# Two attention layers of a two-block transformer: heads in pairs, another order of steps, other PSUM banks, convolution taps loaded from DRAM

## The chip, the cores and the metric

The kernel runs on one core of a Trainium2 chip. The metric is the device time in microseconds of one execution; the kernel before was run three times.

## What is computed

Two transformer blocks run one after the other on 256 tokens of width 1024, in float32. The first block is not touched by the change. The second has two layers, and in each, between two gated feed-forward networks, there is a mixer:

```python
u_conv, q, k, v, q_mem = jnp.split(rms_norm_2(h, mix_norm[l]) @ w_in[l], splits, axis=-1)
y_conv = conv_module(u_conv, ...)      # gate, 31 causal taps per channel (384 channels), layer norm, silu
q = apply_rope(rms_norm_2(q), cos, sin)          # 6 query heads of 64, 2 key/value heads of 64
y_swa = sliding_window_attention(q, k, v, sinks) # blocks of 128, each sees itself and the one before
y_mem = memory_attention(rms_norm_2(q_mem), rms_norm_2(mk), mv)  # 4 heads of 64 over 256 memory rows
h = h + jnp.concatenate([y_conv, y_swa, y_mem], axis=-1) @ w_out[l]
```

## The kernel before, in words

Each engine has its own program in a fixed order, written by hand; semaphores named by `mark` and `at` tie them. All weights come as 268 units of at most 128x2048 floats through three slots. For a unit `u` SyncE loads `raw` when the low part of `u-3` is done, ScalarE writes the high part `w_hi` (`highs`, L888) when TensorE has finished unit `u-3`, VectorE writes the rest `w_lo` (`lows`, L1399), and TensorE multiplies high by high, low by high and high by low (`tile`, L286 to L288; `wide_tile`, L295 to L298; `rows_part`, L331 to L333). Each engine does its units in order, so a `highs` or `lows` call stands at one place in its program, and whatever is ahead of it delays it.

The mixer of a layer, from L706 on TensorE: three convolution units, query/key rows, value and memory-query rows, then memory keys and values. From there to the output projection TensorE alternates between small steps. There are ten heads (`WH`), 0 to 5 with the window, 6 to 9 over the memory:

- `window_scores(i)`: for both query blocks a bfloat16 mask matmul against the identity (L737, window heads only), then queries by keys (L738), on the 64 partitions of that head; a head's scores fill one bank, 0 or 1 by turns.
- VectorE `soft(i)`: row maxima of each query block (L1957, L1961) and the sink (L1964). ScalarE `soft(i)`: exponentials with their sums (L1317).
- `window_turned(i)`: transposes of the exponentials (L747) into bank 2 or 3; ScalarE copies them (L1325); `window_product(i)` multiplies by the values (L762).
- `third_channel(n)`: the convolution's third 128 channels, 31 taps, each a matmul of a diagonal 128x128 matrix with the shifted input (L776). ScalarE makes the diagonals from the identity, four after each head (`diagonals`, L1283), in a ring of eight. The other two thirds are 62 taps on VectorE (`run_taps`, L1916, L1920).

The lines that set the order in the ten rounds are, on ScalarE (behind `soft(i + 2)` and the four diagonals) and on VectorE:

```python
            if i in (1, 3):
                highs(u0 + L_MK + 3 + i // 2)
...
            run_taps(6)
            if i + 2 < WH:
                soft(i + 2)
            if i in (1, 3):
                lows(u0 + L_MK + 3 + i // 2)
```

After the last head, TensorE sums the convolution's channels (`conv_sums`, L828), transposes the memory heads' rows (`rows_turned`, L797), computes the variance (`conv_variance`, L835) and spreads its root (`spread`, L398), between the tiles of the output projection `L_WO`, four units of 16 tiles. The normalised convolution goes through VectorE and ScalarE as one piece of 128x768 (L2024 to L2034, L1372, L1376) and is what chunk 5 of the projection waits for.

## Time and profile before

| | us |
|---|---|
| median of 3 runs (lowest, highest) | 1743.68 (1743.01, 1745.07) |
| the profiled execution | 1742.12 |
| its span in the trace | 1740.8 |
| TensorE busy | 1683.9 |
| VectorE busy | 1232.8 |
| ScalarE busy | 892.8 |
| granted TensorE clock, share of full speed | 0.993 |

Spans and times in the trace count from the start of the profiled execution. A row of a timeline gives the start, the duration, the engine, the line, the operation, and in square brackets the idle time before it with what ended it. A float32 matmul stands as two passes, "x8" is four matmuls merged, and durations of neighbouring passes overlap by some 0.15 us, so what a group costs is read from the start of the next row. The first layer's mixer heads stand at 951 to 1005 us, the second's at 1458 to 1511 us.

### The profile page before, as it was taken

What the parts mean: (1) busy time and instruction counts of PE and PEld (TensorE: products, weight loads), DVE (VectorE), ACT (ScalarE), POOL (GpSimd) and SP (SyncE); (2) the same over time, 40 slices, a digit from 0 to 9 for tenths busy, and PEclk for the clock granted to TensorE, in tenths of its full rate; (3) what the DMA queues carried; (4) which work ended last, traced back from release to release, by engine and by line L of the source; (5) the groups of instructions that cost most, each with busy time, mean ns of one, the idle gap of its engine ahead of it and who ended that gap; (6) DMA issues with size and microseconds to landing.
All of it is one profiled execution on the core that took longest, in us unless ns stands there. A gap on an engine that the chain in (4) does not pass through costs nothing.

```text
span 1740.8 us, 24401 instructions
## 1 busy us (share of the span) xinstructions
PE 1683.9 (97%) x10136; PEld 1487.6 (85%) x10136; DVE 1232.8 (71%) x1487; ACT 892.8 (51%) x1149; POOL 183.2 (11%) x166
## 2 busy tenths in 40 slices
PE   7999999999999999999999899999999999899997
PEld 6889988888998888888889688888888898788886
DVE  7985577765657767677767767778777667677764
ACT  6554455444545554455444555556555545455542
POOL 0401010011101001100021010003100111010002
PEclk9999999999999999999999899999999999999999
DMA  7444345545434555555554215555555542145551
GB/s 280 162 160 143 120 165 194 191 179 211 159 112 166 194 210 182 186 183 190 194 179 149 73 57 210 194 200 189 179 196 187 194 172 107 49 149 189 184 197 55
DMA packets 41439, 291.09 MB, mean 167 GB/s; under 512 B 4720, under 2 KB 4976, under 8 KB 7024
## 3 DMA queue, kind: packets, MB, share of 16 engines
q1 hardware_dynamic: 39456, 282.61, 45.0%
q10 hardware_dynamic: 1872, 6.92, 1.0%
q8 instruction: 80, 1.31, 0.3%
q14 instruction: 31, 0.25, 0.0%
HBM read 288.46 MB, written 1.05 MB: 166 GB/s over the span
## 4 chain that ended last, share of the span: by engine, by line
PE 81%; DVE 11%; ACT 4%; POOL 2%; issue 2%; DMA 0%; ACTq 0%; DVEq 0%; POOLq 0%
PE ps L298 36%; PE ps L297 18%; DVE w_lo L1399 4%; PE ps L295 4%; PE ps L286 3%; PE ps L288 3%; PE ps L287 3%; PE ps L331 2%; PE ps L333 2%; PE ps L332 2%; PE ps L296 2%; DVE xT L1407 2%; ACT w_hi L888 1%; POOL stat L2054 1%; PE ps L437 1%
## 5 line engine op out<-in xcount | busy, mean ns | idle before, releaser
L1399 DVE TENSOR_TENSOR w_lo<-raw,w_hi 128x2048 fp32r<-128x2048 f32 x268 | 613.5, 2292 | 229.8 <-ACT w_hi L888 226.1
L298 PE MATMUL ps<-xT,w_hi 128*128 128x512 f32 x1736 | 620.6, 397 | 0.0
L888 ACT ACTIVATE w_hi<-raw 128x2048 fp32r<-128x2048 f32 x268 | 510.0, 1904 | 215.6 <-PE ps L298 117.7
L297 PE MATMUL ps<-xT,w_lo 128*128 128x256 f32 x1736 | 485.5, 280 | 0.0
L298 PE MATMUL ps<-hT,w_hi 128*128 128x512 f32 x1168 | 412.6, 397 | 0.0
L298 PEld LDWEIGHTS ps<-xT,w_hi 128*128 128x128 f32 x1736 | 326.9, 188 | 67.6
L297 PEld LDWEIGHTS ps<-xT,w_lo 128*128 128x128 f32 x1736 | 328.4, 189 | 11.5
L297 PE MATMUL ps<-hT,w_lo 128*128 128x256 f32 x1168 | 327.2, 280 | 1.7 <-DVE hT L1584 1.7
L298 PEld LDWEIGHTS ps<-hT,w_hi 128*128 128x128 f32 x1168 | 219.3, 188 | 51.0
L297 PEld LDWEIGHTS ps<-hT,w_lo 128*128 128x128 f32 x1168 | 220.3, 189 | 5.0 <-DVE hT L1584 2.9
L940 ACT ACTIVATE tmp<-ps 128x512 f32<-128x512 f32 x120 | 72.0, 600 | 257.5 <-PE ps L298 257.5
L2087 POOL TENSOR_TENSOR ff<-ff 128x256 f32<-128x256 f32 x77 | 98.2, 1275 | 983.2 <-ACT ff L918 668.2
L286 PE MATMUL ps<-xT,w_hi 128*128 128x256 f32 x544 | 158.0, 291 | 4.2 <-DVE xT L2034 2.9
L287 PE MATMUL ps<-xT,w_lo 128*128 128x256 f32 x544 | 154.1, 283 | 0.0
L288 PE MATMUL ps<-xT,w_hi 128*128 128x256 f32 x544 | 154.1, 283 | 0.0
L1458 DVE TENSOR_TENSOR tmp<-ps,tmp 128x512 f32<-128x512 f32 x120 | 82.6, 688 | 86.1 <-ACT tmp L940 85.9
L295 PE MATMUL ps<-xT,w_hi 128*128 128x512 f32 x248 | 100.6, 407 | 16.2 <-DVE w_lo L1614 10.9
L286 PEld LDWEIGHTS ps<-xT,w_hi 128*128 128x128 f32 x544 | 104.6, 192 | 5.0 <-issue 3.3
L287 PEld LDWEIGHTS ps<-xT,w_lo 128*128 128x128 f32 x544 | 104.7, 192 | 0.5
L288 PEld LDWEIGHTS ps<-xT,w_hi 128*128 128x128 f32 x544 | 104.5, 192 | 0.0
L2054 POOL TENSOR_TENSOR stat<-stat,mhalf 128x2 f32<-128x2 f32 (+2 forms) x45 | 47.2, 1055 | 398.4 <-DVE stat L1487 130.9
L331 PE MATMUL ps<-w_hi,memT 128*128 128x256 f32 (+1 forms) x256 | 81.2, 317 | 0.0
(254 smaller groups left out, 2057.4 us busy)
## 6 DMA issues: line engine op xcount, KB each, us to landing
raw<-weights_dram SPq DMA_DIRECT2D x264, 1024.0 KB, 4.8
raw<-weights_dram SPq DMA_DIRECT2D x4, 768.0 KB, 4.1
tmp<-mem_dram ACTq DMA_DIRECT2D x2, 1024.0 KB, 6.6
x<-x_in_dram SPq DMA_DIRECT2D x2, 512.0 KB, 5.8
raw<-weights_dram SPq DMA_DIRECT2D x2, 512.0 KB, 6.7
arena<-mem_dram ACTq DMA_DIRECT2D x1, 1024.0 KB, 7.9
arena<-pool_mat_dram ACTq DMA_DIRECT2D x1, 1024.0 KB, 4.8
tmp<-masks_dram ACTq DMA_DIRECT2D x1, 768.0 KB, 8.4
```

Source lines behind the costliest of these rows:

```text
L286: pe.matmul(out, b.w_hi[:, s, cs], src[:, k, 0, :], start=first, stop=False)
L287: pe.matmul(out, b.w_lo[:, s, cs], src[:, k, 0, :], start=False, stop=False)
L288: return pe.matmul(out, b.w_hi[:, s, cs], src[:, k, 1, :], start=False, stop=last)
L295: pe.matmul(ps[:, bank, :].rearrange("p (a n) -> p a n", a=2), hi, src[:, k, :, :], start=True, stop=False)
L297: pe.matmul(ps[:, bank, 0:S], lo, src[:, k, 0, :], start=False, stop=False)
L298: return pe.matmul(ps[:, bank, :].rearrange("p (a n) -> p a n", a=2), hi, src[:, k, :, :], start=False, stop=last)
L331: pe.matmul(out, h, b.w_hi[:, s, cs], start=(first and j == 0), stop=False)
L888: act.activation(b.w_hi[:, s, 0:w], b.raw[:, s, 0:w], ACT.Copy).then_inc(*mark("hi", u))
L940: act.activation(tmp, ps[:, bank:bank + 2, S:2 * S], ACT.Copy).then_inc(*mark("half", name, j))
L1399: dve.tensor_tensor(b.w_lo[:, s, 0:w], b.raw[:, s, 0:w], b.w_hi[:, s, 0:w].bitcast(F32), ALU.subtract).then_inc(*mark("lo", u))
L1458: dve.tensor_tensor(dst, ps[:, bank:bank + 2, 0:S], tmp, ALU.add).then_inc(*mark(label, *((name, j) if label != "u32" else (name[:-1], j))))
L2087: pool.tensor_tensor(b.acc(), b.sq(0) if c == 1 else b.acc(), b.sq(c), ALU.add).then_inc(*mark("sqsum", f, c))
```

## The change

Heads go in five pairs instead of ten singles, both heads of a pair over one query block at a time. The keys are kept twice, each copy with the other head's 64 partitions at zero, so that one matmul over all 128 partitions gives both heads' scores; GpSimd writes the zeros ahead of time. A column of ones next to the values makes the product give the sums of the exponentials. A pair uses two banks, for scores and, when the exponentials are made, for the transposes. The 31 diagonals come in one transfer of 128x3968 floats from DRAM into `tmp`, issued by ScalarE in the down projection of the first feed-forward network. The orders on TensorE, ScalarE and VectorE are new, and the end of the convolution goes in three pieces.

```diff
     def tap_diagonal(self, j):
-        return self.arena[:, 5, P * (j % 8):P * (j % 8) + P]
+        return self.tmp.rearrange("p a n -> p (a n)")[:, P * j:P * j + P]
...
+class Window:
+    def __init__(self, b):
+        flat = b.flat2(2)
+        self.q = flat[:, 0:768].rearrange("p (k n) -> p k n", k=3)
+        self.k = flat[:, 768:1280].rearrange("p (s n) -> p s n", s=2)
+        self.mq = flat[:, 1280:1792].rearrange("p (k n) -> p k n", k=2)
+        self.mk = b.arena[:, 15, :].rearrange("p (k s n) -> p k s n", k=2, s=2)
...
+    def scores(self, b, pair, t):
+        n = P * self.tiles(pair, t)
+        return b.ps[:, 2 * (pair % 2) + t, 0:2 * n].rearrange("p (s n) -> p s n", s=2)
...
+    def out_projection(u0, f, order, wait_chunk, before=None, first_banks=range(4)):
         for i, ks in enumerate(order):
             u = u0 + i
             pe.wait_ge(*at("lo", u))
+            if i < 3:
+                for j, k in enumerate(ks):
+                    wait_chunk(k)
+                    for bk in first_banks if i + j == 0 else range(4):
+                        out = b.pair(4 + bk)
+                        if before:
+                            before(k, bk)
                         for h in range(2):
+                            last = tile(out[:, h, :], u, 8 * j + 2 * bk + h, b.xT, k, i + j + h == 0, False)
...
         rows_units(u0 + L_QK, ((5,), (6,)), b.xT, 1, 512, 4)
-        rows_units(u0 + L_MQ, ((7,), (3,)), b.xT, 1, 384, 4)
+        pe.wait_ge(*at("factor", mx))
+        rows_units(u0 + L_MQ, ((7,), (4,)), b.xT, 1, 384, 4)
...
         def window_scores(i):
             for t in range(NT):
-                n = P * len(hd["blocks"][t])
-                out = ps[:, bank, S * t:S * t + n]
-                if i in SWA:
-                    pe.matmul(out, b.ident_b[:, :], b.neg_b[:, 1, S * t:S * t + n], start=(t == 0), stop=False)
-                last = pe.matmul(out, hd["q"][:, t * P:t * P + P], hd["k"][:, 0:n], start=(t == 0 and i in MEM), stop=(t == 1))
+                out, n, ts = W.scores(b, i, t), P * W.tiles(i, t), slice(t * P, t * P + P)
+                if i < 3:
+                    neg = b.neg_b[:, 1, S * t:S * t + n].unsqueeze(1).broadcast_to([P, 2, n])
+                    pe.matmul(out, b.ident_b[:, :], neg, start=True, stop=False)
+                    last = pe.matmul(out, W.q[:, i, ts], W.k[:, :, 0:n], start=False, stop=True)
+                else:
+                    last = pe.matmul(out, W.mq[:, i - 3, ts], W.mk[:, i - 3, :, :], start=True, stop=True)
...
-                    pe.wait_ge(*at("factor", mx))
-                pe.wait_ge(*at("tapdiag", l, j))
-                pe.matmul(ps[:, 4, 0:S], b.tap_diagonal(j), yp[:, 2, j:j + S], start=(j == 0),
-                          stop=(j == 30)).then_inc(*mark("tapmm", l, j))
+                    pe.wait_ge(*at("d_diag", l))
+                    pe.wait_ge(*at("vcopy", tag, 1))
+                    pe.wait_ge(*at("hrow", f"mq{l}", 1))
+                i = pe.matmul(ps[:, 4, 0:S], b.tap_diagonal(j), yp[:, 2, j:j + S], start=(j == 0), stop=(j == 30))
...
-        for i in range(WH):
-            window_turned(i)
-            if i == 1:
-                memory_columns("mk", mkr)
-            if i == 3:
-                pe.wait_ge(*at("mkcol", l))
-                memory_columns("mq", qr[:, :, 512:768])
-            if i + 2 < WH:
-                if i == 4:
-                    pe.wait_ge(*at("mqcol", l))
-                window_scores(i + 2)
-            if i < 7:
-                third_channel(4)
-            if i == 1:
-                pe.wait_ge(*at("vcopy", tag, 1))
-                pe.wait_ge(*at("mvcopy", l))
-                pe.wait_ge(*at("hrow", f"mq{l}", 0))
-            if i == 8:
-                pe.wait_ge(*at("third", l))
-                rows_turned(SWA)
-            if i:
-                window_product(i - 1)
-        window_product(WH - 1)
+        window_turned(0)
+        third_channel(2)
+        window_turned(1)
+        pe.wait_ge(*at("vcopy", tag, 1))
+        pe.wait_ge(*at("mvcopy", l))
+        pe.wait_ge(*at("hrow", f"mq{l}", 0))
+        window_product(0)
+        window_scores(2)
+        third_channel(2)
+        window_product(1)
+        pe.wait_ge(*at("mkcol", l))
+        memory_columns("mq", qr[:, :, 512:768])
+        third_channel(4)
+        pe.wait_ge(*at("mqcol", l))
+        window_scores(3)
+        third_channel(2)
+        window_turned(2)
+        third_channel(4)
+        window_product(2)
+        window_scores(4)
+        third_channel(2)
+        window_turned(3)
+        third_channel(3)
+        rows_turned(SWA)
+        window_product(3)
+        window_turned(4)
+        third_channel(31)
+        window_product(4)
...
+            if k in (0, 3):
+                pe.wait_ge(*at("olo", tag, 2 * k))
+            elif k >= 5:
+                pe.wait_ge(*at("yclo", l, k - 5))
+        def before(k, bk):
+            if (k, bk) == (0, 0):
+                rows_turned(MEM)
+                pe.wait_ge(*at("third", l))
+            if (k, bk) == (1, 2):
                 conv_sums()
+            if (k, bk) == (2, 3):
+                conv_variance()
+            if (k, bk) == (3, 3):
                 spread(f"conv{l}", 1)
+        out_projection(u0 + L_WO, fb, ((0, 1), (2, 3), (4, 5), (6, 7)), chunk, before, (2, 3, 0, 1))
...
+        def load_diagonals(dn):
+            if dn == 0:
+                act.wait_ge(*at("hlo", fa, FF2_UPS - 1))
+                act.dma_start(b.tmp.rearrange("p a n -> p (a n)")[:, 0:31 * P], d["tap_diagonals"][l]).then_inc(*landed("d_diag", l))
+        feed_forward(fa, u0 + L_FFA, True, mx, load_diagonals)
...
-        def diagonals(n):
-                if j >= 8:
-                    act.wait_ge(*at("tapmm", l, j - 8))
-                act.activation(b.tap_diagonal(j), b.c("ident"), ACT.Copy,
-                               scale=b.lp("conv_w")[:, 3 * j + 2:3 * j + 3]).then_inc(*mark("tapdiag", l, j))
...
+        def sides(dst, src, scale=1.0):
+            for side in range(2):
+                ss = slice(64 * side, 64 * side + 64)
+                i = act.activation(dst[ss, side, :], src[ss, :], ACT.Copy, scale=scale if scale == 1.0 else scale[ss, :])
+            return i
...
-                e = act.activation(pb[:, t, 0:n], ps[:, i % 2, S * t:S * t + n], ACT.Exp, bias=nm, accum_out=den)
+                src, n = W.scores(b, i, t), P * W.tiles(i, t)
+                for side in range(2):
+                    at0 = W_NM + WH * t + 2 * i + side
+                    e = act.activation(W.p[i % 2][:, t, side, 0:n], src[:, side, :], ACT.Exp, bias=b.stat[:, at0:at0 + 1])
...
+        highs(u0 + L_MK + 3)
         soft(0)
         soft(1)
...
-        for i in range(WH):
-            turned_copy(i)
-            if i == 1:
-                memory_columns("mk", mkt)
-            if i == 3:
-                act.wait_ge(*at("mq_gain", l))
-                memory_columns("mq", qkt[:, 4:6, :])
-            if i + 2 < WH:
-                soft(i + 2)
-            if i == 5:
...
-            if i < 6:
-                diagonals(4)
-            if i in (1, 3):
-                highs(u0 + L_MK + 3 + i // 2)
-            if i == 6:
-                act.wait_ge(*at("tapmm", l, 30))
-                act.activation(yc[:, 2, :], ps[:, 4, 0:S], ACT.Identity, bias=b.lp("conv_b")[:, 2:3]).then_inc(*mark("third", l))
+        turned_copy(1)
+        memory_keys()
+        memory_queries()
+        soft(2)
+        turned_copy(2)
+        soft(3)
+        act.wait_ge(*at("sinkarg", l))
...
+        highs(u0 + L_MV + 3)
+        turned_copy(3)
+        soft(4)
         act.wait_ge(*at("otr", l, SWA.start))
+        turned_copy(4)
+        act.wait_ge(*at("third_sum", l))
+        act.activation(yc[:, 2, :], ps[:, 4, 0:S], ACT.Identity, bias=b.lp("conv_b")[:, 2:3]).then_inc(*mark("third", l))
+        act.wait_ge(*at("otr", l, MEM.start))
...
+        conv_sigmoid(0)
+        conv_sigmoid(1)
+        conv_high(0)
+        conv_sigmoid(2)
+        conv_high(1)
+        conv_high(2)
...
-        run_taps(4)
+        run_taps(7)
         lows(u0 + L_QK + 3)
-        run_taps(4)
+        run_taps(6)
...
-        run_taps(2)
+        head_norms(f"mk{l}", [W.mk_rows[:, t, :] for t in range(NT)], [ps[:, 5, HALVES[t]] for t in range(NT)],
+                   [W.mk_junk[:, t, :] for t in range(NT)], 4, 64, 64, EMM, ("ms_m", f"mem2_{l}"))
...
+                m = dve.tensor_reduce(nm[:, t, :], W.scores(b, i, t), AX.X, ALU.max, negate=True)
+            if i < 3:
+                m.then_inc(*mark("rowmax", tag, i))
+                dve.wait_ge(*at("neg_sink", l))
+                dve.wait_ge(*at("rowmax", tag, i))
+                sink = b.stat[:, W_NSINK + 2 * i:W_NSINK + 2 * i + 2].unsqueeze(1).broadcast_to([P, NT, 2])
+                m = dve.tensor_tensor(nm, nm, sink, ALU.min)
...
-        for i in range(WH):
-            run_taps(6)
-            if i + 2 < WH:
-                soft(i + 2)
-            if i == 4:
-                sink_arguments()
-            if i in (1, 3):
-                lows(u0 + L_MK + 3 + i // 2)
-            if i == 7:
-                normalized_rows(SWA)
+        lows(u0 + L_MQ + 4)
+        run_taps(15)
+        soft(2)
+        run_taps(11)
+        soft(3)
+        sink_arguments()
+        lows(u0 + L_MK + 3)
+        run_taps(6)
+        soft(4)
+        normalized_rows(SWA)
+        run_taps(5)
+        lows(u0 + L_MV + 3)
+        run_taps(4)
+        row_lows(SWA)
+        run_taps(4)
+        normalized_rows(MEM)
         run_taps(62)
-        row_lows(SWA)
+        row_lows(MEM)
...
+        lows(u0 + L_WO + 3)
         dve.wait_ge(*at("spread", f"conv{l}"))
-        dve.tensor_tensor(yc, yc, ps[:, 1, 0:S].unsqueeze(1).broadcast_to([P, 3, S]), ALU.mult).then_inc(*mark("cnormed", l))
-        dve.wait_ge(*at("cnormed", l))
         for k in range(3):
-        lows(u0 + L_WO + 3)
+            dve.tensor_tensor(yc[:, k, :], yc[:, k, :], ps[:, 1, 0:S], ALU.mult).then_inc(*mark("cnormed", l, k))
+        for k in range(3):
...
+        conv_gate(0)
+        conv_gate(1)
+        conv_low(0)
+        conv_gate(2)
+        conv_low(1)
+        conv_low(2)
...
+        W = Window(b)
+        for zeros in (W.k, W.mk):
+            pool.memset(zeros, 0.0)
+        for ones in (W.v, W.mv):
+            fill = pool.memset(ones[:, :, :, 64:65], 1.0)
+        fill.then_inc(*mark("window_fill", l))
...
+        diagonals[l, np.arange(P), :, np.arange(P)] = i["conv_w_2"][l][:, 2 * P:].T
```

The first place is ScalarE within the heads of a layer, where L1317/L1334 are the exponentials, L1325/L1342 the copies of the transposes, L1332/L1356 the memory columns, L1283 the diagonals. Before:

```order
L1325 ACTIVATE arena<-ps 128x384 [waits pt]
L1332 ACTIVATE arena<-ps,par 128x256 [waits ctr]
L1332 ACTIVATE arena<-ps,par 128x256
L1317 ACTIVATE arena,stat<-ps,stat 128x128 [waits pt,mx]
L1317 ACTIVATE arena,stat<-ps,stat 128x256
L1283 ACTIVATE arena<-cst,par 128x128 [waits tapmm,d_par]
L1283 ACTIVATE arena<-cst,par 128x128 [waits tapmm] x3
L888 ACTIVATE w_hi<-raw 128x2048 [waits unit,d_w1]
L1325 ACTIVATE arena<-ps 128x384 [waits pv,pt]
```

and with the change:

```order
L1342 ACTIVATE arena<-ps 128x2x384 [waits pv,pt]
L1334 ACTIVATE arena<-ps,stat 128x256 [waits pt,mx]
L1334 ACTIVATE arena<-ps,stat 128x256 x3
L1377 ACTIVATE stat<-stat 128x12 [waits sinkarg]
L907 ACTIVATE w_hi<-raw 128x2048 [waits unit,d_w2]
L1342 ACTIVATE arena<-ps 128x1024 [waits pv,pt]
L1334 ACTIVATE arena<-ps,stat 128x256 [waits pt,mx]
```

The diagonals are gone from between, and the high part (L888, now L907) stands ahead of the copy of the fourth pair; the one before it moved ahead of the first exponentials.

The second place is VectorE in the same stretch, where L1961 or L1989 are the row maxima and L1920 or L1951 the taps. Before:

```order
L1920 SCALAR_TENSOR_TENSOR arena<-arena,par 128x256 [waits vector_step] x6
L1961 TENSOR_REDUCE stat<-ps 128x1 [waits sc]
L1961 TENSOR_REDUCE stat<-ps 128x1
L1964 TENSOR_SCALAR stat<-stat,par 128x2 [waits vector_step]
L1399 TENSOR_TENSOR w_lo<-raw,w_hi 128x2048 [waits hi]
L1920 SCALAR_TENSOR_TENSOR arena<-arena,par 128x256 [waits vector_step] x6
```

and with the change:

```order
L1429 TENSOR_TENSOR w_lo<-raw,w_hi 128x2048 [waits hi]
L1951 SCALAR_TENSOR_TENSOR arena<-arena,par 128x256 [waits vector_step] x15
L1989 TENSOR_REDUCE stat<-ps 128x2 [waits sc]
L1989 TENSOR_REDUCE stat<-ps 128x2
L1995 TENSOR_TENSOR stat<-stat 128x2x2 [waits vector_step,neg_sink]
L1951 SCALAR_TENSOR_TENSOR arena<-arena,par 128x256 [waits vector_step] x11
```

A block of taps between two maxima is 15 or 11 long where it was 6, and the low part stands ahead of that block and no longer directly behind the fourth head's maxima.

## Rows read from the trace of the kernel before

**Rows 1.** The page's first part: busy time of each engine.

```profile
PE 1683.9 (97%) x10136; PEld 1487.6 (85%) x10136; DVE 1232.8 (71%) x1487; ACT 892.8 (51%) x1149; POOL 183.2 (11%) x166
```

**Rows 2.** Busy time by stretch: length, PE, PEld, DVE, ACT, POOL, clock, DMA share, GB/s.

```profile
957.00:1003.60 46.60, 39.97 (x207) 31.54 (x206) 34.56 (x82) 24.79 (x74) 1.98 (x2) 0.89 0.19 68
```

**Rows 3.** What TensorE waited for, first layer, 905 to 1060: total, times, longest.

```profile
PE ps L776 <- ACT arena L1283: 5.8, 3, 3.7
PE ps L286 <- DVE xT L2034: 1.5, 1, 1.5
...
PE ps L797 <- DVE arena L1989: 1.3, 2, 0.8
```

**Rows 4.** The same, second layer, 1410 to 1560.

```profile
PE ps L776 <- ACT arena L1283: 6.8, 3, 3.7
```

**Rows 5.** Timeline of TensorE, first layer's heads.

```profile
951.42 0.23 PE L737 MATMUL ps<-neg_b,ident_b 128*128 128x128 bf16 x1
...
952.84 0.23 PE L737 MATMUL ps<-neg_b,ident_b 128*128 128x128 bf16 x1
...
969.20 2.00 PE L776 MATMUL ps<-arena 128*128 128x256 f32 x8
971.03 0.78 PE L762 MATMUL ps<-arena 128*128 128x64 f32 x6
...
971.98 0.60 PE L788 MATMUL ps<-cst,arena 128*128 128x128 f32 x4
...
977.58 3.78 PE L776 MATMUL ps<-arena 128*128 128x256 f32 x8 [3.68 <-ACT arena L1283]
...
983.10 1.13 PE L738 MATMUL ps<-arena 64*128 64x256 f32 x4
984.15 2.00 PE L776 MATMUL ps<-arena 128*128 128x256 f32 x8
...
990.06 3.56 PE L776 MATMUL ps<-arena 128*128 128x256 f32 x8 [1.90 <-ACT arena L1283]
993.46 0.78 PE L762 MATMUL ps<-arena 128*128 128x64 f32 x6
```

**Rows 6.** Timeline of TensorE, second layer's heads and projection.

```profile
1484.47 3.51 PE L776 MATMUL ps<-arena 128*128 128x256 f32 x8 [3.69 <-ACT arena L1283]
...
1489.02 1.13 PE L738 MATMUL ps<-arena 64*128 64x256 f32 x4
...
1506.94 0.85 PE L797 MATMUL ps<-cst,arena 128*128 128x128 f32 x6 [0.79 <-DVE arena L1989]
...
1528.44 0.36 PE L286 MATMUL ps<-xT,w_hi 128*128 128x256 f32 x1 [1.48 <-DVE xT L2034]
```

**Rows 7.** Timeline of VectorE, first layer's heads.

```profile
970.83 2.29 DVE L1399 TENSOR_TENSOR w_lo<-raw,w_hi 128x2048 fp32r<-128x2048 f32 x1 [3.94 <-ACT w_hi L888]
973.03 2.46 DVE L1920 SCALAR_TENSOR_TENSOR arena<-arena,par 128x256 f32<-128x256 f32 x6
...
976.06 0.23 DVE L1964 TENSOR_SCALAR stat<-stat,par 128x2 f32<-128x2 f32 x1
```

**Rows 8.** Timeline of ScalarE, the same stretch.

```profile
967.73 1.27 ACT L1283 ACTIVATE arena<-cst,par 128x128 f32<-128x128 f32 x4
...
976.32 0.37 ACT L1317 ACTIVATE arena<-ps,stat 128x128 f32<-128x128 f32 x1 [5.16 <-DVE stat L1964]
```

**Rows 9.** TensorE's groups by form: line, operation, shapes, count, busy, mean ns, idle before.

```profile
L417 PE MATMUL ps<-neg_b,ident_b 128*128 128x512 bf16 x4 | 1.5, 382 | 0.0
L398 PE MATMUL ps<-ff,cst 128*128 128x512 f32 x2 | 1.1, 621 | 0.0
```

**Rows 10.** DMA issues: size each, median us to landing.

```profile
tmp<-mem_dram ACTq DMA_DIRECT2D x2, 1024.0 KB, 6.6
```

**Rows 11.** Timeline of GpSimd ahead of the first layer's heads.

```profile
934.20 3.24 POOL L2054 TENSOR_TENSOR stat<-stat,mhalf 128x8 f32<-128x8 f32 x2 [21.41 <-DVE stat L1487]
```

**Rows 12.** GpSimd's groups by form.

```profile
L2117 POOL TENSOR_TENSOR arena<-arena 128x1024 f32<-128x1024 f32 x1 | 2.5, 2536 | 0.0
```

270 lines of the change are left out of this document (115 added, 155 removed).

## Prediction

> **What bounds the kernel now.** I read the page's first part, then the windows, then what TensorE waited for, then the timelines of the stretch that the change touches. The first part shows TensorE busy for 97% of the span [rows 1], so time can only come from TensorE's own work, its clock or the little idle time it has. By windows, one stretch stands out: from 957.0 to 1003.6 TensorE is busy for 39.97 of 46.60 us at a granted clock of 0.89, while VectorE has 34.56 us of work and ScalarE 24.79 [rows 2]. So nobody is full there: three engines hand small pieces to each other.
>
> The waits name the place. In the first layer TensorE waits 5.8 us for ScalarE's diagonals, 1.5 us for the last part of the convolution and 1.3 us for normalised rows [rows 3]; in the second 6.8 us for the diagonals [rows 4], and as long as in the first for the other two, of which 1.48 and 0.79 us stand in the timeline [rows 6]. The timeline shows the price of the long gaps: after 3.68 us of idling, taps, a product and transposes take from 977.58 to 983.10, 5.52 us, where the same steps took 2.78 us from 969.20 to 971.98; TensorE has fallen from the 2.4 GHz level to the 1.2 GHz one [rows 5]. After the 1.90 us gap eight passes take 3.40 us (990.06 to 993.46) instead of 1.83 (969.20 to 971.03) [rows 5]. In the second layer the same steps take 4.55 us from 1484.47 to 1489.02 behind a gap of 3.69 us [rows 6].
>
> Why the gap? TensorE lacks diagonals, but ScalarE makes them behind a head's exponentials. Those it could start only at 976.32, after 5.16 us of idling for VectorE's maxima [rows 8]. VectorE gave them at 976.06, since ahead of them stood a low part for whose high part it had idled 3.94 us, to 970.83, and six taps [rows 7]. And ScalarE made that high part behind earlier exponentials and four diagonals, at 967.73 [rows 8]. It is a ring: each waits for something that stands late in another's order.
>
> **The change, part by part, for one layer.**
>
> *The ring.* The diagonals leave ScalarE (31 of some 0.3 us, 1.27 for four [rows 8]), and with them TensorE's 31 waits. The high parts stand ahead of the first exponentials and behind the fourth pair's, VectorE finds them ready. I laid the new order out by hand from 951.42, each step at the start-to-start time of its like: four taps 1.83 us, three products 0.62, three transposes 0.33, a low part 2.20, and for six VectorE taps 2.46 less the overlap, 2.38 [rows 5, 7]. TensorE then reaches the third pair's transposes at 973.5, their exponentials are there at 971.0; the window heads' rows at 982.3 against 981.7; the first product 0.15 us before the memory values are copied, the only wait. So the diagonal waits go: 5.8 us in the first layer, 6.8 in the second.
>
> *VectorE.* It becomes the next late one. Its work in the window of 46.60 us is 34.56 us [rows 2]; three taps of 0.40 us and the memory key rows (some 2 us) move ahead, one low part of 2.2 us moves in, pairing saves some 1.5. That leaves some 32 us; with some 4 us of waiting for scores it ends the taps near 993 to 994. TensorE needs them at `conv_sums`, now 12 tiles into the projection, near 996.5. The cover is 2.5 us. The five taps moved ahead of the query norms cost nothing: VectorE idled there for high parts and roots.
>
> *The tail.* The projection takes the place of the waits for rows (1.3 us) and for the last part of the convolution (1.5 us) [rows 3, 6]: variance and spread stand 10 and 8 tiles apart, a tile being 0.36 us, and only the first third of the convolution has to be there for chunk 5. By my layout it comes at 1009.6 and is asked for at 1009.7. Both waits go; this is the tightest place.
>
> *The clock.* Without gaps of over a microsecond there is nothing behind which it fell. This gives back 2.74 + 1.57 = 4.3 us in the first layer [rows 5] and 4.55 - 2.78 = 1.8 us in the second [rows 5, 6].
>
> *The scores.* A window head took 1.42 us (951.42 to 952.84), a memory head 1.05 (983.10 to 984.15) [rows 5]. The new pair streams the same columns over 128 partitions in half the instructions. A float32 pass over 512 columns is not in the heads; the nearest rows are a pass of 621 ns and a bfloat16 one of 382 ns [rows 9], less the overlap (a 256 pass of 0.38 us stands 0.23 from the next, 1.83 / 8): 0.47 us and some 0.3. A window pair is a mask and two passes for either block, 0.2 + 2 x 0.23 + 0.3 + 2 x 0.47 = 1.9 us, and with some 0.2 us for changing between mask and float32 2.1 us, instead of 2.84. A memory pair is 4 x 0.47 = 1.9 instead of 2.1. Three and two of them save 2.6 us. The bounds are nothing saved at all, and 3.4 us if the changes cost nothing and a 512 pass twice 0.23. I take 2.6, as the 621 ns row is of this very form.
> The trace shows 64-partition passes of one head and of the next strictly one behind the other. The Trainium skill's TensorEngine Tiling (Array Packing), section Key Properties, says that changing the tiling mode drains TensorE; by it the 0.2 us would vanish too, for the new order stays in one mode, and the sum would be 1 us larger over both layers. The same page's speedup of up to 2 for two 64-row tiles side by side would speak against padding to 128 rows, but the heads before show no such overlap (1.42 us each, one after the other), so the padding gives up nothing that was had.
>
> *What is added elsewhere.* The table is 2 MB a layer on ScalarE's queue. A 1 MB load into the same buffer at the same point of another down projection landed in 6.6 us [rows 10], with no wait of TensorE beside it; the taps come eleven units of 16 tiles, some 60 us, later. GpSimd's zeros are 1536 elements per partition; two inputs of 1024 took it 2.5 us [rows 12], and it idles 21.41 us before the roots [rows 11]. Without that cover they would cost 13 and 4 us a layer.
>
> **The sum.** Waits 8.6 + 9.6 = 18.2; clock 4.3 + 1.8 = 6.1; scores 5.2; together 29.5 us. I take off 0.5 us a layer for the copy of the values and for one more change between projection and small steps: 28.5 us. The profiled execution took 1742.12 us, so 1713.6; the median of the runs stands 1.6 us above it, which gives **1715 us**.
>
> **Rivals.**
> - *One gap a layer stays.* Another order has another late step: a pair's maxima behind 15 taps, or the tail's 0.1 us margin. For it: margins of 0.1 to 2.5 us, worked out from durations read to 0.1. Against it: they add up in no place that I found. Price, as the first gap: 3.68 + 2.74 = 6.4 us a layer, thus 1728.
> - *Padding saves nothing.* The scores cost what they did: 1715 + 5.2 = 1720.
> - *Slower: the pairs run in series.* Only two are under way, and scores and transposes share banks, so a pair's scores wait for the product before. If VectorE's maxima come late each time, three pairs a layer idle as the first gap did: 3 x 6.4 = 19.2 us against 14.2 gained, so 5 us lost a layer and 1743.7 + 10 = 1754. It decides from 14.2 / 6.4 = 2.2 such gaps a layer. Against it: VectorE's idle time in the stretch, 12 of 46.6 us [rows 2].
> - *The change doesn't do what it says:* the table comes in late and TensorE waits for it at the first tap instead. It would need over 60 us for 2 MB where 2 x 6.6 = 13.2 is what the row gives; I give it nothing.
> - *More than forecast:* half as many steps in the stretch also means some 20 fewer changes between kinds of matmul, at up to 0.1 us each, and no residue: 1708.
>
> **How the numbers follow.** The forecast with the bounds of its scores and without residue (1712 to 1720) 0.61, which takes in the second rival; more than that, down to 1708, 0.08; one gap a layer, up to 1728, 0.22; between that and no change 0.05; slower 0.04. A measurement here tells 0.2%, 3.5 us, from no change. Faster 0.94, same 0.02, slower 0.04. The range for 8 in 10 is 1708 to 1728, which leaves out some 0.1.
>
> **What would show it.** Right: no wait of TensorE over 0.5 us between 951 and the end of the projection; the heads' clock at 1.00; the first feed-forward matmul behind the mixer some 14 us earlier in each layer, everything else as before; a window pair's scores near 2.1 us. The clock step is wrong if the heads still show passes at twice their length. VectorE's step is wrong if `conv_sums` waits for taps. The prediction is wrong if any wait on maxima or exponentials of over a microsecond stands in the heads, or if weights come late in the feed-forward networks.

## The result, and the profile after

The changed kernel takes 1707.49 us (median of 4 runs, 1704.65 to 1708.97) against 1744.38 us before on the same chip: a ratio of 0.9775, 95% interval 0.976 to 0.979. The forecast was 1715.0 us with a range from 1708 to 1728. The sign came out, and most of the mechanism, but 37 us were gained and not 29. The runs spread over 4 us, so on which side of 1708 their median falls is chance; the 8 us of surplus are not. The profiled execution took 1706.11 us, 36.0 less than the profiled one of before.

The page's first part, which answers to [rows 1]:

```profile
PE 1666.4 (98%) x10081; PEld 1477.1 (87%) x10084; DVE 1230.3 (72%) x1483; ACT 872.9 (51%) x1053; POOL 193.9 (11%) x174
```

TensorE is busy for 17.5 us less (which includes what it lost to the slower clock) and idles less, with almost the same number of instructions. The windows (length, PE, PEld, DVE, ACT, POOL, clock, DMA share, GB/s) cover the heads and the projection of the first layer, and the heads of the second:

```profile
950.65:988.20 37.55, 37.40 (x230) 31.29 (x229) 34.48 (x74) 19.78 (x40) 1.98 (x2) 1.00 0.28 95
988.20:1015.00 26.80, 26.80 (x218) 26.43 (x218) 16.82 (x33) 13.96 (x19) 1.69 (x3) 1.00 0.20 72
1439.79:1477.30 37.51, 37.36 (x230) 31.25 (x228) 34.47 (x74) 19.77 (x40) 1.98 (x2) 1.00 0.26 95
```

In the heads TensorE is busy for 37.40 of 37.55 us at a clock of 1.00, where in [rows 2] it was 39.97 of 46.60 us at 0.89. VectorE, with 34.48 us, is now the next full engine. All that TensorE waited for from 945 to 1060 us (total, times, longest), where [rows 3] had 5.8, 1.5 and 1.3 us:

```profile
PE ps L390 <- POOL ff L2129: 1.6, 1, 1.6
PE ps L771 <- issue: 0.2, 1, 0.2
```

The 1.6 us stand in the feed-forward network behind the mixer, where [rows 3] leaves out waits of 1.3 and 0.3 us.

**Where the time went.** I measure the changed stretch from the start of the first mask to the start of the first feed-forward matmul behind the projection, and call it the stage. Before it took 83.29 us in the first layer (951.42 to 1034.71) and 81.72 us in the second; now 64.37 us (950.65 to 1015.02) and 64.38 us. That is 18.9 + 17.3 = 36.3 us, the whole gain. By idle time in front of TensorE's rows it splits into 17.9 us of waits (8.63 + 9.61 became 0.15 + 0.15) and 18.3 us of work that takes less time. The forecast had 18.2 us of waits, and of the rest only 11.3 (clock 6.1, scores 5.2) less 1.0 of residue. So the surplus lies in the work. The scores show it at once. TensorE's first two window pairs, and further on a memory pair between taps:

```profile
950.65 0.28 PE L746 MATMUL ps<-neg_b,ident_b 128*128 128x256 bf16 x1
950.77 0.60 PE L747 MATMUL ps<-arena 128*128 128x256 f32 x2
951.21 0.38 PE L746 MATMUL ps<-neg_b,ident_b 128*128 128x512 bf16 x1
951.42 1.02 PE L747 MATMUL ps<-arena 128*128 128x512 f32 x2
952.28 0.27 PE L746 MATMUL ps<-neg_b,ident_b 128*128 128x256 bf16 x1
...
968.30 1.88 PE L749 MATMUL ps<-arena 128*128 128x512 f32 x4
970.02 1.03 PE L787 MATMUL ps<-arena,tmp 128*128 128x256 f32 x4
970.88 0.82 PE L758 MATMUL ps<-cst,arena 128*128 128x128 f32 x6
```

A window pair takes 952.28 - 950.65 = 1.63 us, not the 2.1 of the forecast; a memory pair 970.02 - 968.30 = 1.72, not 1.9. A pass over 512 columns takes 1.72 / 4 = 0.43 us, and a pass over 256 columns (970.88 - 970.02) / 4 = 0.215. Nothing is lost between a mask and a matmul: from 950.77 to 951.21 the two passes behind the first mask take 0.44 us.

### The profile page after: what moved, and what is told of

Its sections match the earlier page's. It is cut to its first block, busy times and chain, and to the rows that moved or that the text cites. A ratio compares the mean times of both kernels' runs of the same rounds, so it can differ in the third digit from the quotient of the medians.

```text
span 1704.8 us, 24182 instructions
## 1 busy us (share of the span) xinstructions
PE 1666.4 (98%) x10081; PEld 1477.1 (87%) x10084; DVE 1230.3 (72%) x1483; ACT 872.9 (51%) x1053; POOL 193.9 (11%) x174
## 4 chain that ended last, share of the span: by engine, by line
PE 86%; DVE 8%; ACT 2%; POOL 2%; issue 1%; DMA 0%; POOLq 0%; ACTq 0%; DVEq 0%
PE ps L302 37%; PE ps L301 19%; PE ps L299 4%; PE ps L290 3%; DVE w_lo L1429 3%; PE ps L292 3%; PE ps L291 3%; PE ps L335 2%; PE ps L337 2%; PE ps L336 2%; PE ps L300 2%; PE ps L787 2%; DVE xT L1437 1%; PE ps L771 1%; ACT w_hi L907 1%
## 5 line engine op out<-in xcount | busy, mean ns | idle before, releaser
L907 ACT ACTIVATE w_hi<-raw 128x2048 fp32r<-128x2048 f32 x268 | 510.1, 1904 | 198.0 <-PE ps L302 117.9
L301 PEld LDWEIGHTS ps<-xT,w_lo 128*128 128x128 f32 x1736 | 328.5, 189 | 11.3
L2129 POOL TENSOR_TENSOR ff<-ff 128x256 f32<-128x256 f32 x77 | 102.5, 1331 | 971.9 <-ACT ff L937 668.1
L2096 POOL TENSOR_TENSOR stat<-stat,mhalf 128x2 f32<-128x2 f32 (+2 forms) x45 | 50.7, 1132 | 361.8 <-DVE stat L1517 111.9
## 6 DMA issues: line engine op xcount, KB each, us to landing
tmp<-tap_diagonals_dram ACTq DMA_DIRECT2D x2, 1984.0 KB, 11.1
```

Source lines behind the costliest of these rows:

```text
L301: pe.matmul(ps[:, bank, 0:S], lo, src[:, k, 0, :], start=False, stop=False)
L907: act.activation(b.w_hi[:, s, 0:w], b.raw[:, s, 0:w], ACT.Copy).then_inc(*mark("hi", u))
L2129: pool.tensor_tensor(b.acc(), b.sq(0) if c == 1 else b.acc(), b.sq(c), ALU.add).then_inc(*mark("sqsum", f, c))
```

## Experiments on the scores

A "row" here is a partition of the operands: the scores of one head use 64 of them, the other matmuls of the stretch 128. Theory 1: each stretch of 64-row matmuls between 128-row ones costs some 0.2 us for going there and back. Rivals: a 64-row pass is itself slow, or the column price alone differs. The first kernel below is the control.

Where no interval is given, a kernel ran once. What counts then is its stage, read from its own trace. The whole time is less sure, since two runs can differ in clock falls outside the stage. split128 and half64_grouped below are 3.7 us apart in their stages, both layers together, and 0.6 us in their times: in split128 the clock fell once more in the feed-forward networks and once more early in the first block.

**split128.**

```
-  last = pe.matmul(out, W.q[:, i, ts], W.k[:, :, 0:n], ...)
+  for side in range(2):
+      ss = slice(0, P)
+      q, k = (W.q[ss, i, ts], W.k[ss, side, 0:n]) ...
+      last = pe.matmul(out[:, side, :], q, k, ...)
```

> The changed kernel, each side's scores in a matmul of their own (256 columns over 128 zero-padded rows instead of both sides as 512 columns). The control for the next two. If TensorE's price is by columns alone (theory 1), a pair's scores stay at 1.63 us (window) and 1.72 us (memory) and the stage from the first mask to the feed-forward network's first matmul stays at 64.4 us. If one 512 column pass is cheaper than two of 256 columns (rival), each pair grows by 0.1 us or more and the stage by some 0.5 to 1 us.

Measured: 1707.66 us, stage 64.45 and 64.44 us. Columns alone set the price; the number of instructions doesn't.

**half64.** Here `ss` is `slice(0, 64)` for side 0.

> The split form again, with side 0 over its own 64 rows and side 1 over 128: ten lone 64-row matmuls a layer between 128-row ones. Theory 1 (going from 128 rows to 64 and back costs some 0.2 us, whatever stands between): 10 x 0.2 = 2.0 us more a layer than the split form, a window pair at 2.0 us, the stage at 66.4 us. Theory 2 (a 64-row pass is itself slower, by 0.19 / 4 = 0.05 us as a memory head's 1.05 us for four passes suggests): 20 passes x 0.05 = 1.0 us more a layer, 65.4 us. The forecast's own reckoning (the change between mask and matmul costs, rows don't): nothing more, 64.4 us.

Measured: 1715.38 us, stage 68.29 us in both layers, 3.85 more than the control, or 0.385 us for each of the ten stretches, nearly twice the 0.2 of theory 1. The timeline shows the same pair as above, with 64-row matmuls merged into rows with their 128-row neighbours, and a memory pair:

```profile
952.11 0.28 PE L746 MATMUL ps<-neg_b,ident_b 128*128 128x256 bf16 x1
952.33 0.90 PE L750 MATMUL ps<-arena 64*128 64x128 f32 x4
953.07 0.38 PE L746 MATMUL ps<-neg_b,ident_b 128*128 128x512 bf16 x1
953.38 1.32 PE L750 MATMUL ps<-arena 64*128 64x256 f32 x4
954.54 0.27 PE L746 MATMUL ps<-neg_b,ident_b 128*128 128x256 bf16 x1
...
972.24 2.58 PE L750 MATMUL ps<-arena 64*128 64x256 f32 x8
974.65 1.03 PE L788 MATMUL ps<-arena,tmp 128*128 128x256 f32 x4
```

From mask to matmul 0.22 us pass instead of 0.12 (952.11 to 952.33, against 950.65 to 950.77 above): 0.10 us are paid on the way in, and the rest on the way out. The pair takes 2.43 us instead of 1.63.

**half64_grouped.** Masks and side 1 of both blocks first, then side 0 of both.

> The same matmuls as half64, but in each pair the masks and side 1 of both blocks first, then side 0 of both: five 64-row stretches a layer instead of ten, the same 20 passes. Theory 1 (a price for each stretch): 5 x 0.2 = 1.0 us above the split form, stage 65.4 us, half of what half64 adds. Theory 2 (a price for each 64-row pass): as much as half64 adds. The forecast's reckoning: nothing.

Measured: 1708.25 us, stage 66.29 us in both layers: 1.85 us above the control, 0.37 for each of five stretches, and half of what half64 adds with the same passes. That excludes the slow pass. The price belongs to the change of the row count; what the engine does in that time no run shows.

**b_both_grouped** asks whether this holds in the old kernel's order and banks. It is b_both (told below), with both masks of a window head ahead of its two matmuls.

> b_both (the kernel before with table and high parts ahead) with both masks of a window head ahead of its two 64-row matmuls: 6 + 4 = 10 stretches of 64 rows a layer instead of 12 + 4 = 16, the same matmuls and columns. Theory 1 (0.37 us for each stretch, as in half64 and half64_grouped): 6 x 0.37 = 2.2 us less a layer, stage 73.04 to 70.8 us, 1717.7 us in all. If the price belongs to the changed kernel's banks or order (rival): the stage stays within 0.5 us of 73.0.

Measured: stage 72.23 us, so 0.81 less and not 2.2; 1720.87 us against 1722.14. TensorE's work in the stage (its length less the waits) fell by 1.72 us (70.24 to 68.52), 0.29 for each of six stretches, but TensorE now waited 0.90 us more for exponentials. So the price exists there too, and half of it went into a new wait.

The two prices, 0.385 and 0.29, belong to two kinds of stretch, and the trace of the kernel before shows both. Its first head:

```profile
951.58 0.49 PE L738 MATMUL ps<-arena 64*128 64x128 f32 x2
952.00 0.28 PE L737 MATMUL ps<-neg_b,ident_b 128*128 128x256 bf16 x1
952.21 0.70 PE L738 MATMUL ps<-arena 64*128 64x256 f32 x2
```

Two passes of 128 columns take 952.00 - 951.58 = 0.42 us, where columns alone would take 0.22, and the mask behind them 0.21 us where it takes 0.12 in the changed kernel: 0.2 us on the way out and 0.1 on the way in, 0.30 for a stretch with a mask behind it. With float32 matmuls behind it another 0.1 us stands in their row (four taps 1.83 instead of 1.73 us), 0.40 in all. The six stretches that b_both_grouped removes all had a mask behind them (0.29 measured), the ten of half64 all a float32 matmul (0.385), and half64_grouped has one of the first kind and four of the second: 0.30 + 4 x 0.385 = 1.84 us against 1.85 measured.

**tap_marks.** Four taps take 1.73 us now (1.83 before, [rows 5]). I held the semaphore mark and wait of each tap for the cause and put them back.

```
+  pe.wait_ge(*at("d_diag", l))
   i = pe.matmul(ps[:, 4, 0:S], b.tap_diagonal(j), ...)
+  if j < 30:
+      i.then_inc(*mark("tapmm", l, j))
```

> The changed kernel, with a wait on the table and a semaphore mark at each of the third channel's 31 taps again, both idle. If the marks made a tap dearer (four taps 1.83 us before, 1.73 us after), four taps take 1.83 us again and the stage grows by 31 x 0.025 = 0.7 to 0.8 us a layer, to 65.1 us. If the saving came from the table's place or the diagonals' maker, it stays at 64.4 us.

Measured: 1706.02 us, stage 64.37 and 64.36 us, all taps together 13.4 us as without marks. That theory fell: the waits and marks of 31 taps cost nothing. What carries the difference is the way out of the 64-row scores, behind which taps used to stand. half64_grouped shows it: there three pairs end on 64-row matmuls with taps behind, and a layer's taps take 13.70 us instead of 13.40, 0.10 us for each of the three places. In b_both, told below, seven groups of taps stand behind 64-row scores, and a layer's taps take 14.13 us.

## Experiments on the ring

Theory 2 is the forecast's: orders that wait for each other make the gaps, and the diagonals are only the last link. The other theory is that ScalarE has too much to do with 31 diagonals; the expectations call it theory 1, and it has nothing to do with the theory 1 of the scores.

**b_table.** The kernel before, with diagonals from the table and `diagonals()` empty.

> The kernel before, with one part of the change: the third channel's diagonals come from a table by DMA, and ScalarE makes none. Order, heads and tail are the old ones. Theory 1 (the waits hang on the diagonals themselves): the waits of 5.8 and 6.8 us go, and with them the clock's 4.3 and 1.8 us, so some 18.7 us less, 1725 us. Theory 2 (the ring of orders is the cause, and the diagonals only its last link): VectorE still idles for the high part, the third head's exponentials still come late, and TensorE waits for them in place of the diagonals, 2 to 3.5 us a layer; half or less of the 18.7 us comes, 1732 us or more.

**b_ahead.** The kernel before, with its high parts ahead:

```
+  highs(u0 + L_MK + 3)
   soft(0)
   soft(1)
...
-  if i in (1, 3):
-      highs(u0 + L_MK + 3 + i // 2)
+  if i == 2:
+      highs(u0 + L_MK + 4)
```

> The kernel before, with another part alone: ScalarE makes the first of the two high parts ahead of the first exponentials and the second one head earlier. ScalarE still makes the diagonals in its ring of eight. Theory 2 (ring of orders): VectorE finds the high part ready, its 3.94 us of idling go, and the first gap of TensorE (3.68 us in both layers) shrinks below 1 us; some 8 us less or more in all, 1734 us. Theory 1 (ScalarE's 31 diagonals themselves are too much for it): the waits for diagonals stay at 4 us a layer or more, and the time within 3 us of before.

**b_both.** Both.

> Both parts on the kernel before: table and high parts ahead, but heads one by one, 64 rows, old tail. If ring and clock are as forecast, the heads have no wait over 0.5 us and the clock stays at 1.00: 12.6 + 6.1 = 18.7 us less, 1725 us, and the two waits of the tail (1.3 and 1.5 us a layer) stay. The rest of the change's gain, 37 - 18.7 = 18 us, would then be pairs, rows and tail.

Measured, beside 1742.27 us for the kernel before: b_table 1734.86, b_ahead 1727.45, b_both 1722.14 us. TensorE's waits from 945 to 1040 us with the table alone:

```profile
PE ps L747 <- ACT arena L1314: 2.6, 1, 2.6
PE ps L286 <- DVE xT L2031: 1.5, 1, 1.5
PE ps L798 <- DVE arena L1986: 1.3, 2, 0.8
PE ps L295 <- DVE w_lo L1396: 1.3, 1, 1.3
PE ps L738 <- ACT arena L1329: 0.6, 1, 0.6
```

The waits for diagonals are gone and TensorE waits for exponentials instead (L1314, then L1329), 3.2 us a layer. With the high parts ahead alone, from 945 to 1060 us:

```profile
PE ps L797 <- DVE arena L1990: 1.3, 2, 0.8
PE ps L776 <- ACT arena L1283: 0.7, 2, 0.4
PE ps L738 <- ACT arena L1332: 0.5, 1, 0.5
```

Here 0.7 us are left of 5.8, though ScalarE still makes every diagonal. VectorE finds the high part ready, where in [rows 7] it had idled 3.94 us:

```profile
956.43 0.23 DVE L1965 TENSOR_SCALAR stat<-stat,par 128x2 f32<-128x2 f32 x1
956.57 2.28 DVE L1400 TENSOR_TENSOR w_lo<-raw,w_hi 128x2048 fp32r<-128x2048 f32 x1
```

Moving two calls brings 14.8 us of the 20.1 that both parts bring, the table alone 7.4; by the stages, both layers together, it is 16.0 and 6.6 of 18.9 us. In b_both the only wait left in the heads is the 0.80 us for their normalised rows, which b_both keeps, and the clock is 1.00:

```profile
950.66:997.00 46.34, 45.54 (x273) 37.00 (x272) 39.83 (x92) 21.05 (x64) 1.98 (x2) 1.00 0.19 69
```

Its stage is 73.04 us in both layers, 10.25 + 8.68 = 18.9 us less than before, where 18.7 were forecast for ring and clock. 12.6 of them are waits (8.63 + 9.61 less twice 2.80), and the other 6.3 the clock, forecast at 6.1. In b_ahead, where ScalarE still makes the diagonals, the same reckoning gives 5.8.

**a_ring.** The changed kernel, with ScalarE's ring of eight.

```
-  pe.wait_ge(*at("d_diag", l))
+  pe.wait_ge(*at("tapdiag", l, j))
...
   memory_keys()
+  diagonals(3)
   memory_queries()
+  diagonals(2)
   soft(2)
+  diagonals(4)
```

> The changed kernel with the diagonals made by ScalarE again, in the old ring of eight, in pieces of 2 to 5 behind the steps of the new order; the table isn't loaded. Theory 1 (the table matters): ScalarE, busy 19.8 of 37.6 us now, gets 31 x 0.3 = 9.3 us more, its exponentials and copies come up to 1 us later each, and TensorE waits 3 us a layer or more, 1713 us or more. Theory 2 (the order matters): waits stay under 1 us a layer and the time within 2 us of the changed kernel's.

Measured: 1708.00 us, stage 66.03 us, with one wait of 1.40 us on ScalarE in a layer. So in the new order the table is worth 1.66 us a layer by the stages, and 0.5 to 2 us in all by the times (the changed kernel's two medians are 1707.49 and 1706.05), where in the old order it brought 3.3 us a layer by the stages and 7.4 in all by the times. That lies between the theories' numbers and nearer to the second: the order carries most of the gain.

## Experiments on the margins

**a_tail_one.** The convolution's end in one piece, and `pe.wait_ge(*at("yclo", l, 2))` for every chunk from 5.

> The changed kernel with the convolution's end in one piece again: gate, high part and low part over all three chunks, and TensorE waits for the whole before chunk 5. Everything else as changed. If the thirds carry the tail, as forecast, TensorE asks for chunk 5 at 1006.4 us and gets it at some 1007.9 (gate 0.96, high part 0.84, low part 0.96 us behind 1005.0): a wait of 1.5 us a layer, the stage 65.9 us. If the earlier place of conv_sums, variance and spread alone moved the tail ahead (rival), the wait is under 0.5 us.

Measured: 1708.49 us, stage 66.17 us, and this wait ahead of the projection's chunk 5:

```profile
PE ps L290 <- DVE xT L2077: 1.8, 1, 1.8
```

So the thirds do carry the tail; moving the sums ahead alone would have kept the old wait of 1.5 us.

**a_late17** makes the third pair's maxima late by force. That is the slower rival's first step; no taps are left to make the later pairs' maxima late as well.

```
-  run_taps(15)
+  run_taps(32)
   soft(2)
-  run_taps(11)
   soft(3)
```

> The changed kernel with 17 more of VectorE's taps (15 + 17 = 32) ahead of the third pair's maxima. This is the slower rival's case by force: maxima end near 972.2 us, exponentials 1.35 us later near 973.6, asked for at 971.0. If one late step costs its own gap and the clock behind it, TensorE waits 2.6 us a layer and passes behind the gap take up to twice their length, 2 to 3.7 us more (as behind the 2.6 us gap of the kernel before with the table): 4.6 to 6.3 us a layer, 1717 to 1720 us. If the pairs ran in series behind it (rival: each later pair late as well), over 8 us a layer, above 1723 us. If gaps are absorbed (another rival), under 2 us a layer.

Measured: 1714.63 us. TensorE waits 2.44 us in both layers, once; the later pairs are not late. The stage grew by 2.64 us in the first layer (67.01) and by 4.32 in the second (68.70), both less than the 4.6 to 6.3 expected. The windows behind the gap, first and second layer:

```profile
975.00:980.50 5.50, 5.50 (x31) 4.33 (x32) 2.00 (x1) 4.17 (x7) 0.00 (x0) 1.00 0.37 143
1466.00:1471.50 5.50, 5.50 (x27) 4.71 (x26) 1.46 (x1) 4.17 (x7) 0.00 (x0) 0.73 0.56 188
```

The same gap, the same steps behind it, and the clock fell in one layer and not in the other (0.73 is the mean of a window that holds stretches at both levels).

## Versions meant to beat both

**a_pool7_4.** GpSimd takes eleven taps, each in two instructions:

```
+  for ch, count in ((2, 7), (1, 4)):
+      for n in range(count):
+          pool.tensor_scalar(side, yp[:, ch, j:j + S], cw[...], None, ALU.mult)
+          pool.tensor_tensor(dst, dst, side, ALU.add)
```

> A version meant to beat both: GpSimd, idle 46.5 us from 953 to 999.6 in the changed kernel, takes the last 7 taps of the third channel and the last 4 of the second (a multiplication and an addition each); TensorE adds the first partial sum by one matmul with the identity, VectorE the second by one addition. TensorE saves 7 - 1 = 6 matmuls of 0.43 us = 2.6 us a layer, VectorE 4 - 1 = 3 taps of 0.4 us, so that its taps end 1.2 us earlier. If GpSimd does a tap in 2 x 1.3 us = 2.7 us beside VectorE, its 11 taps end near 983, in time for both: 2.6 us less a layer, 1702.3 us. Rival: VectorE is slowed by GpSimd beside it (a tap of more than 0.45 us instead of 0.40), its taps end after conv_sums asks for them, and the gain is under 1.5 us a layer or a loss.

Measured: 1720.92 us, ratio to before 0.9857 (0.983 to 0.9884), 13 us slower than the changed kernel. GpSimd was quicker than thought (a tap in 1.9 us, all eleven done at 974.0), but VectorE lost. Its timeline, with 15 and 11 taps beside GpSimd and 6 behind it:

```profile
957.96 9.49 DVE L1952 SCALAR_TENSOR_TENSOR arena<-arena,par 128x256 f32<-128x256 f32 x15
...
968.74 6.30 DVE L1952 SCALAR_TENSOR_TENSOR arena<-arena,par 128x256 f32<-128x256 f32 x11
...
978.44 2.45 DVE L1952 SCALAR_TENSOR_TENSOR arena<-arena,par 128x256 f32<-128x256 f32 x6
```

A tap takes 0.57 to 0.63 us beside GpSimd (11 in 6.30 us, 15 in 9.49) and 0.40 alone (15 took 6.02 us in the changed kernel). The Trainium skill's SBUF — State Buffer, section Who interferes with whom, says that a VectorE operation with both inputs in SBUF and a GpSimd operation reading it exclude each other. The taps are of this kind, and the trace agrees as far as VectorE is slowed. GpSimd's multiplications took 0.97 us beside taps, and one took 2.96 us while VectorE's low part of 2.28 us ran. The heads' rows came late, and TensorE paid with a gap and, as the double length of the next steps shows, with the clock:

```profile
983.54 1.54 PE L811 MATMUL ps<-cst,arena 128*128 128x128 f32 x6 [3.25 <-DVE arena L2019]
984.88 3.52 PE L771 MATMUL ps<-arena 128*128 128x65 f32 x16
```

**a_sums_later.** The changed kernel waits 1.6 us a layer in the second feed-forward network for GpSimd's squares, the first row of its waits above. Its windows right behind that wait and one step on:

```profile
1022.80:1027.25 4.45, 4.45 (x19) 3.80 (x19) 4.45 (x5) 0.39 (x1) 1.99 (x1) 0.62 0.85 326
1027.25:1030.00 2.75, 2.75 (x17) 2.42 (x16) 0.62 (x3) 0.00 (x0) 0.70 (x1) 1.00 0.95 352
```

In the kernel before, waits of 1.3 and 0.3 us (for a low part and for the spread) stood there instead. The sum is the same, but the change has made one gap of two, and that matters to the clock. Behind the 1.3 us it did not fall, in the kernel before nor in any run that has this wait. Behind the 1.6 us it fell in 8 of 18 places (two layers in each of nine runs), and a fall costs some 1.7 us: in the first layer eight tiles behind the wait took 4.43 us where the next eight took 2.77. The changed kernel's second run, in the same place, had no fall:

```profile
1022.80:1027.25 4.45, 4.45 (x27) 3.92 (x27) 4.45 (x5) 0.30 (x1) 2.07 (x1) 1.00 0.90 337
```

The edit:

```
-  if j == 0:
+  between = {(0, 1): (4, after_first), (1, 0): (6, after_second)}.get((j, i)) if later else None
+  if j == 0 and not later:
       (after_second if i else after_first)()
```

> The changed kernel with the second feed-forward networks' column sums 5 tiles into the second unit instead of ahead of it, and the spread 7 tiles into the third. TensorE no longer waits 1.6 us a layer for GpSimd's sums of squares; behind that wait one unit's first eight tiles took 4.43 us where the next eight took 2.77, so up to 3.2 us a layer could come back: 1701 us. Rival: the low part of the second unit is ready only near 1021.7 us, asked for at 1020.8, and TensorE waits 1 us for it instead: 0.7 us a layer or less, 1706 us.

**a_taps2.** Taps 29 and 30 of the third channel on VectorE:

```
-  others = iter(range(31))
+  others = iter(range(29))
...
+  dve.tensor_tensor(yc[:, 2, :], ps[:, 4, 0:S], yc[:, 2, :], ALU.add)
```

> The changed kernel with the third channel's last two taps on VectorE, which also adds TensorE's sum and the bias in place of ScalarE. TensorE saves 2 x 0.43 = 0.86 us a layer; VectorE, whose taps end 2.05 us before they are asked for, gets 2 x 0.40 + 0.42 = 1.2 us more, which fits by 0.0 us (992.2 against 992.2). Gain 0.9 us a layer at most, 1705.7 us; half of it if VectorE's steps in the heads come late by the 0.8 us.

**a_sums_taps2.**

> Both of these together. If they don't touch each other: the sum of the two gains, at best 3.2 + 0.9 = 4.1 us a layer, 1699 us; by the rival of the first 1704 us.

Measured, ratios to before: a_sums_later 1702.98 us (0.976, 0.9744 to 0.9777), a_taps2 1703.73 (0.9765, 0.9751 to 0.978), both 1702.00 (0.9754, 0.9739 to 0.9768). The profiled spans, 1704.8 for the changed kernel, are 1701.6, 1703.1 and 1699.8 us. The two taps give 0.87 us a layer in the stage (63.50), as worked out, with no new wait. For the sums the rival's wait came as it said:

```profile
1021.65 0.50 PE L299 MATMUL ps<-xT,w_hi 128*128 128x512 f32 x1 [1.02 <-DVE w_lo L1433]
...
1022.30:1027.25 4.95, 4.95 (x32) 4.38 (x31) 4.95 (x5) 0.77 (x1) 2.10 (x1) 1.00 0.84 316
```

(The second line is the window behind it.) By the medians 3.1 to 4.5 us came back, more than the rival's 0.7 us a layer. The shorter gap gives 0.6 us a layer. The clock gives the rest as far as a trace shows it: it stayed at 1.00 behind all six gaps of 1.0 us in the three runs with this edit, and fell behind 8 of 18 of 1.6 us.

**after_again and best_again**: the changed kernel and a_sums_taps2 side by side.

> The changed kernel once more, beside the next one on the same chip. Its stage at 64.4 us in both layers again and its time within 0.1% of 1707.5 us, if the session before was typical; if that session was a slow or fast one, the time moves by over 2 us while the stages stay.

> The version with later column sums and two taps on VectorE, once more. By the profiled spans (1699.8 against 1704.8 us) it should be 5 us faster than the changed kernel, by the rival (the spans are chance) less than 2 us.

Measured: 1706.05 us (1704.72 to 1707.46; ratio to before 0.9778, 0.9762 to 0.9794) and 1701.11 us (1699.62 to 1701.23; 0.9747, 0.9732 to 0.9763). The version with both edits is 4.9 us faster than the changed kernel, and its runs all lie below those of the changed one. It is the fastest found here.

## Why the prediction was wrong, and where it was right

- **The ring: right.** Both parts of it were isolated, and each wait of the forecast went: 17.9 us, where 18.2 less the residue of 1.0 were forecast. ScalarE's order was the main cause: b_ahead alone took the first layer's wait for diagonals from 5.8 to 0.7 us.
- **The clock: right in size.** 5.8 us by b_ahead and 6.3 by b_both, against 6.1. Not foreseen was the single gap of 1.6 us in the second feed-forward network: "everything else as before" did not hold there, and in the profiled run it brought a clock fall of its own in the first layer.
- **VectorE's cover: right.** The only wait in the heads is the 0.15 us ahead of the first product, as said. VectorE ends the taps at 991.0 and `conv_sums` starts at 993.05: 2.05 us of cover against 2.5. a_taps2 spent it without a wait.
- **The tail: right, and tight as said.** The first third is ready at 1006.23 us and chunk 5 starts at 1006.29. a_tail_one makes it a wait of 1.8 us.
- **Table and fills: right.** The table's 1984 KB landed in 11.1 us, unseen; no wait on it stands anywhere.
- **The scores: the step that failed.** "Three and two of them save 2.6 us. The bounds are nothing saved at all, and 3.4 us" a layer. From b_both to the changed kernel TensorE's work in the stage fell from 70.24 to 64.22 us, 6.0 us a layer, of which 4.5 to 4.7 in the scores' own rows, 0.7 in the taps' behind them and 0.4 in the transposes' ahead of them. Three things were off. The 512 pass was priced at 0.47 us from a row's length less an overlap, where twice the 256 pass would have been right. I added 0.2 us a pair, for which no row stood, for the change between mask and matmul, which costs nothing. And the main one: the change between 64 and 128 rows had no term of its own. It stood beside the sum alone, as 0.2 us that "would vanish too", 0.5 us a layer; in truth it is paid in and out of all 16 stretches (12 in window heads, 4 in memory heads). Seven of them have a mask behind, at 0.30 us, and nine a float32 matmul, at 0.385 to 0.40: 5.6 to 5.7 us a layer, of the 6.0. The other 0.3 to 0.4 stand mostly in the projection's rows and have no experiment. Over both layers TensorE's steps, the clock apart, gave 12.0 us, where the scores' term was 5.2. With waits of 17.9 us (17.2 forecast, when the residue is taken off) and the clock's 6.3 (6.1) this makes 6.8 + 0.7 + 0.2 = 7.7 of the surplus of 7.8 us (36.3 by the stages against 28.5).
- **The bound on it** was no bound: it was built from columns at 0.23 us, a figure from taps behind 64-row scores that already held 0.1 us of the way out, and so the range's low end inherited the error. The rival "more than forecast" named some 20 changes between kinds of matmul, at up to 0.1 us, a price that no row gives; what counted were 16 stretches of another row count, at three to four times that. That the result lies near its 1708 is luck.
- **The slower rival** fell: in the changed kernel no pair waits at all. With the third pair's maxima late by force only that pair waits, so one late step costs its gap and perhaps a clock fall, and starts no series. Maxima late at every pair were not tried.

The Trainium skill's TensorEngine Tiling (Array Packing), section Key Properties, says that changing the tiling mode drains TensorE. The runs agree, and give the change a size: 0.30 us for a 64-row stretch with a mask behind it, 0.385 to 0.40 us with float32 matmuls behind it. Two 64-row matmuls side by side, the packing that the prediction weighed against padding, were not tried.

## What to carry to other kernels

When two engines wait for each other's pieces, look for the one call that stands too early or too late in a third engine's order before taking work away: moving two calls gave twice as much as removing 31 instructions. Padding a contraction from 64 to 128 rows cost no time here and saved the change at each end; count the switches of row count in a stage and price them by an experiment, not by a guess from neighbouring rows. An idle engine is no gift: measure what it does to its neighbours before moving work to it. And when a change moves waits about, look at the longest single one and not only at their sum, since the clock may fall behind it.

## What the runs showed of the hardware

- A 64-row stretch among 128-row matmuls costs 0.385 us beyond its columns when a float32 matmul follows (half64) and 0.29 when a bfloat16 mask matmul follows (b_both_grouped).
- A wait on a semaphore that has long been reached, on each of 31 matmuls, and a mark on 30 of them cost nothing (stage 64.37 us with and without, tap_marks).
- VectorE's float32 taps took 0.57 to 0.63 instead of 0.40 us while GpSimd multiplied and added in SBUF (a_pool7_4).
- Whether the clock falls behind a gap is not settled by its length alone. It fell behind 8 of 18 gaps of 1.6 us, one of two of 2.44 us (a_late17) and both of 3.7 us in the kernel before, but not behind the one of 2.87 us in its second layer (1496.95 us), nor behind two of 1.77 us (a_tail_one), nor behind any of the twelve of 1.3 us and six of 1.0 us. What decides stays open.
